# VectorE's modulation columns take their weight block one slab earlier

## The chip, the cores and the metric

The kernel runs on one core of one Trainium2 chip. The metric is the device time of one execution in microseconds (us). The time before is the median of three runs.

## The reference

Two blocks of a network, one after the other, each of two layers. Batch 1, 512 tokens of width 1024, and 256 context tokens beside them in the first block. All in float32.

The first block's layer `l`, cut to what matters here (the context goes the same way, with `c_ctx` in place of `c`; layer 1 leaves the context's output out):

```python
mx = jnp.split((jax.nn.silu(c) @ w_ada[l] + b_ada[l])[:, None, :], 6, axis=-1)
hx = modulate(rmsnorm(x, g_pre_mix[l]), mx[0], mx[1])          # h * (1 + scale) + shift
out_x, out_c = token_mixers(hx, hc, w_in[l], w_out[l], ...)
x = x + mx[2] * rmsnorm(out_x, g_post_mix[l])
hx = modulate(rmsnorm(x, g_pre_mlp[l]), mx[3], mx[4])
x = x + mx[5] * rmsnorm(jnp.square(jax.nn.relu(hx @ w_mlp1[l])) @ w_mlp2[l], g_post_mlp[l])
```

`w_ada[l]` is 1024 x 6144, `w_mlp1[l]` 1024 x 4096, `w_mlp2[l]` 4096 x 1024. The second block has the same kind of modulation, `mod = silu(c_2) @ ada_w_2[l] + ada_b_2[l]` with `ada_w_2[l]` 1024 x 3072, in front of three mixing branches, and no MLP.

## The kernel before

**Layout.** Activations lie transposed, features on the 128 partitions, tokens along the row. A matmul in full float32 is made of three faster ones: weights and activations are both split into a rounded part and the rest, and high x high, rest x high and high x rest are added in PSUM (L1104, L1105, L1106). A weight *slab* is up to 128 x 1024 numbers (512 KB). It comes from HBM into one of the six places of the ring `RG` (`RING = 6`; `RGR` is the same memory). ScalarE rounds it, half by half, into one of the two buffers `WHI` (L2321), GpSimd leaves the rest in place, in `RGR` (L2749).

**The transfer queue.** SyncE asks for all slabs in the order in which the schedule made them. For slab `i` it first waits until the last user of slab `i - 6` is done: a matmul (`matmuls`), or a column on VectorE (`columnsV`):

```python
if i >= RING:
    older = o.slabs[i - RING]["last"]
    e.wait_ge(*at("columnsV" if o.pieces[older]["kind"] == "column" else "matmuls", older))
e.dma_start(RG[:, i % RING, 0:n], dram["W"][i, :, 0:n])     # L1006
```

**The MLP.** Each layer of the first block does its MLP in four rounds of two stages: a `w_mlp1` stage (kind `relu2`, activations `HR`, 8 slabs) and a `w_mlp2` stage (kind `plus`, activations `HIDR`, 8 slabs). In layer 0 a slab is multiplied for 256 context tokens and then for 512 tokens (24 matmuls of each length, two pieces), in layer 1 for 512 tokens alone. After a `relu2` piece ScalarE empties the PSUM bank with a relu into `RLT` (L2483), VectorE squares it (L1861), ScalarE rounds the square into `HIDR` (L2485), VectorE makes the rest (L1863). After a `plus` piece VectorE adds the bank to `OUTF` (L1871 in the first round, L1874). Four PSUM banks serve in turn.

**The columns.** Part of the modulation is computed on VectorE during the MLPs. One column is 128 outputs of a modulation: the slab is a transposed block of `w_ada` or `ada_w_2`, 128 outputs by 1024 inputs, and VectorE multiplies it with the silu of `c`, spread over all partitions, and sums along the row. In layer 0 there are 48 columns with two products each, for `c` and for `c_ctx` (L1656, L1659); in layer 1 there are 36 with one (L1663). They are needed only after the MLP.

**What sets the order.** One list of steps is written by a schedule (`Order`), and each engine's program goes through it and takes the steps that concern it. After every piece `run` adds that piece's estimated time to `credit`; when `credit` reaches the period (8.0 in layer 0, 5.0 in layer 1), `filling` calls `next_column`. With estimates of 8.4 and 5.6 per slab this is once after each weight slab, behind its last evacuation. `next_column` puts a column's step into the list and makes the slab of a later one (`column`, which appends to `loaded`; `sums` holds those whose slab is not made yet). Slabs of weights and columns thus alternate in the ring. The weight slab after the one at work is made before the work on it begins. ScalarE's and GpSimd's rounding of a slab's halves (`split`) is put into the list by `place`, from estimates of when a buffer and a ring place are free. In layer 1 VectorE also makes tables of sine and cosine arguments between the pieces (`table`, L2050 to L2063).

Of the kernel before, what the change touches and what calls it, by code (L numbers as in the profile page):

```python
# [143 lines left out]
class Order:  # L144
# [88 lines left out]

    def next_column(self):

        if self.loaded and (len(self.loaded) > 1 or not self.sums):
            self.step("column", self.loaded.pop(0))
        if self.sums:
            self.column(*self.sums.pop(0))
# [2663 lines left out]
```

## Time and profile before

| | |
|---|---|
| runs | 3344.07, 3338.84, 3344.05 us; median 3344.05 |
| the profiled execution | 3338.16 us, its span 3336.40 us |
| mean granted TensorE clock | 0.945 |
| TensorE busy | 3000.8 us (90%) |
| VectorE busy | 1596.7 us (48%) |
| ScalarE busy | 1056.0 us (32%) |
| GpSimd busy | 1187.9 us (36%) |
| moved | 276.98 MB, mean 83 GB/s |

The profile is of one execution of the program. PE is TensorE's matmuls, PEld its weight loads, DVE VectorE, ACT ScalarE, POOL GpSimd, SP SyncE; SPq is SyncE's issuing of a transfer. Times count from the start of the span. L12 is line 12 of the kernel. A tile's buffer number is left out. The clock is the share of full speed that TensorE was granted. In layer 0 the MLP runs from 530 to 1153 us, in layer 1 from 1560 to 1994 us.

### The profile page before, as it was taken

The numbers are of one execution on the slowest core, as the hardware profiler recorded it, in microseconds if no ns is written. First come the engines' busy times: TensorE is split into PE (matmuls) and PEld (weight loads), VectorE is DVE, ScalarE is ACT, GpSimd is POOL, SyncE is SP. The second block draws the span as 40 slices with busy tenths as digits, with TensorE's granted clock in tenths as the row PEclk, the third lists the DMA queues.
The fourth block names the chain that finished last, engine by engine and source line by source line (L and its number), as shares of the span: only waits on it lengthen the run. The fifth ranks groups of instructions, "written<-read, shape, count | busy, mean of one in ns | idle before, by whom it ended". The sixth has DMA issues, their size and how long they took to land.

```text
span 3336.4 us, 41550 instructions
## 1 busy us (share of the span) xinstructions
PE 3000.8 (90%) x15908; PEld 2412.6 (72%) x15908; DVE 1596.7 (48%) x2851; ACT 1056.0 (32%) x1958; POOL 1187.9 (36%) x862
## 2 busy tenths in 40 slices
PE   7999788898899989968879899999989999999898
PEld 5788677777778867857657676777678767776786
DVE  4673535545555257344533214553482245544822
ACT  3224434121212231344222233233333322333332
POOL 1121142333333422214434452333255623332555
PEclk9999898999999989978989998999999989999999
DMA  5232011323233211103434321212112312221222
GB/s 202 90 138 76 13 55 53 102 101 109 94 114 107 66 57 63 58 23 101 145 106 154 119 89 67 74 64 64 61 60 73 93 64 70 64 70 57 62 75 67
DMA packets 78388, 276.98 MB, mean 83 GB/s; under 512 B 8544, under 2 KB 10848, under 8 KB 77936
## 3 DMA queue, kind: packets, MB, share of 16 engines
q1 hardware_dynamic: 75824, 268.91, 24.3%
q10 hardware_dynamic: 2368, 5.42, 0.4%
q8 instruction: 128, 2.10, 0.3%
q14 instruction: 68, 0.56, 0.1%
HBM read 272.19 MB, written 2.10 MB: 82 GB/s over the span
## 4 chain that ended last, share of the span: by engine, by line
PE 67%; DVE 15%; DMA 6%; ACT 5%; issue 4%; POOL 2%; SPq 0%; DVEq 0%; ACTq 0%; POOLq 0%
PE pb L1104 14%; PE pb L1105 14%; PE pb L1106 14%; DMA RG<-in_W_dram 6%; PE pb L1231 2%; DVE RLT L1861 2%; PE pb L1126 2%; PE pb L1128 2%; PE pb L1127 2%; PE pb L1143 1%; DVE AR L1822 1%; PE pb L1144 1%; PE pb L1145 1%; POOL RGR L2749 1%; PE pb L1189 1%
## 5 line engine op out<-in xcount | busy, mean ns | idle before, releaser
L2749 POOL TENSOR_TENSOR RGR<-RG,WHI 128x512 fp32r<-128x512 f32 x708 | 1002.5, 1426 | 1863.3 <-ACT WHI L2321 1862.3
L2321 ACT ACTIVATE WHI<-RG 128x512 fp32r<-128x512 f32 x708 | 432.5, 623 | 858.9 <-DMA RG<-in_W_dram 434.2
L1104 PE MATMUL pb<-HI,WHI 128*128 128x512 f32 (+1 forms) x880 | 374.8, 426 | 10.5 <-DVE LO L1750 4.9
L1106 PE MATMUL pb<-LO,WHI 128*128 128x512 f32 (+1 forms) x880 | 351.7, 400 | 0.0
L1105 PE MATMUL pb<-HI,RGR 128*128 128x512 f32 (+1 forms) x880 | 351.2, 399 | 0.0
L1104 PE MATMUL pb<-HR,WHI 128*128 128x512 f32 (+1 forms) x768 | 287.3, 374 | 68.0 <-POOL RGR L2749 61.6
L1104 PE MATMUL pb<-HIDR,WHI 128*128 128x512 f32 (+1 forms) x768 | 280.5, 365 | 42.4 <-POOL RGR L2749 17.1
L1106 PE MATMUL pb<-HR,WHI 128*128 128x512 f32 (+1 forms) x768 | 283.7, 369 | 0.0
L1105 PE MATMUL pb<-HR,RGR 128*128 128x512 f32 (+1 forms) x768 | 283.5, 369 | 0.0
L1105 PE MATMUL pb<-HIDR,RGR 128*128 128x512 f32 (+1 forms) x768 | 278.2, 362 | 0.0
L1106 PE MATMUL pb<-HIDR,WHI 128*128 128x512 f32 (+1 forms) x768 | 278.1, 362 | 0.0
L1861 DVE TENSOR_TENSOR RLT<-RLT 128x256 f32<-128x256 f32 (+1 forms) x96 | 98.2, 1023 | 270.0 <-ACT RLT L2483 269.4
L1104 PEld LDWEIGHTS pb<-HR,WHI 128*128 128x128 f32 x768 | 151.0, 197 | 105.7 <-issue 79.1
L1104 PEld LDWEIGHTS pb<-HI,WHI 128*128 128x128 f32 (+1 forms) x880 | 166.8, 190 | 77.9 <-issue 32.2
L1104 PEld LDWEIGHTS pb<-HIDR,WHI 128*128 128x128 f32 x768 | 147.0, 191 | 75.0 <-issue 28.4
L1106 PEld LDWEIGHTS pb<-LO,WHI 128*128 128x128 f32 (+1 forms) x880 | 166.5, 189 | 43.4
L1105 PEld LDWEIGHTS pb<-HI,RGR 128*128 128x128 f32 (+1 forms) x880 | 167.1, 190 | 38.4 <-issue 4.3
L1104 PE MATMUL pb<-HH,WHI 128*128 128x512 f32 (+1 forms) x464 | 170.8, 368 | 13.2 <-DVE HL L1750 12.1
L1106 PEld LDWEIGHTS pb<-HR,WHI 128*128 128x128 f32 x768 | 151.2, 197 | 24.0
L1105 PEld LDWEIGHTS pb<-HR,RGR 128*128 128x128 f32 x768 | 151.6, 197 | 22.7
L1105 PE MATMUL pb<-HH,RGR 128*128 128x512 f32 (+1 forms) x464 | 165.2, 356 | 0.0
L1106 PE MATMUL pb<-HL,WHI 128*128 128x512 f32 (+1 forms) x464 | 165.2, 356 | 0.0
(418 smaller groups left out, 5696.3 us busy)
## 6 DMA issues: line engine op xcount, KB each, us to landing
RG<-in_W_dram SPq DMA_DIRECT2D x504, 512.0 KB, 3.6
XCX<-in_xT_dram ACTq DMA_DIRECT2D x4, 512.0 KB, 11.8
out_dram<-XCX SPq DMA_DIRECT2D x8, 256.0 KB, 2.1
CS<-in_CST_dram ACTq DMA_DIRECT2D x1, 1027.0 KB, 4.8
XCC<-in_ctxT_dram SPq DMA_DIRECT2D x4, 256.0 KB, 13.7
AR<-in_VEC_dram ACTq DMA_DIRECT2D x1, 1024.0 KB, 6.3
CS<-in_CST_dram SPq DMA_DIRECT2D x1, 523.0 KB, 4.3
RG<-in_W_dram SPq DMA_DIRECT2D x2, 256.0 KB, 3.0
```

The costliest lines, as they stand in the source:

```text
L1104: e.matmul(out, hi[:, k, :], xh, start=k == order[0], stop=False)
L1105: e.matmul(out, lo[:, k, :], xh, start=False, stop=False)
L1106: i = e.matmul(out, hi[:, k, :], xl, start=False, stop=k == order[7])
L1126: e.matmul(out, xh[:, sl], hi[:, k, :], start=h == 0 and i0 % per == 0 and k == 0, stop=False)
L1127: e.matmul(out, xh[:, sl], lo[:, k, :], start=False, stop=False)
L1128: i = e.matmul(out, xl[:, sl], hi[:, k, :], start=False, stop=p["final"] and ends and k == nk - 1)
L1143: e.matmul(out, hi[:, k, :], xh, start=k == 0, stop=False)
L1144: e.matmul(out, lo[:, k, :], xh, start=False, stop=False)
L1231: m = e.matmul(sum_at(tag, c), squares_at(tag, i)[:, a:a + 128], ones[:, 0:1], start=k == 0 and c == first, stop=k == 7 and c == 5)
L1861: e.tensor_tensor(r, r, r, MUL).then_inc(*up("evacV", ("hidden", i)))
L2321: e.activation(WHI[:, u % 2, h * n:h * n + n], RG[:, s % RING, h * n:h * n + n], ACT.Copy).then_inc(*up("weightsA", (u, h)))
L2749: e.tensor_tensor(RGR[:, s % RING, sl], RG[:, s % RING, sl], WHI[:, u % 2, sl].bitcast(F32), SUB).then_inc(*up("weightsG", (u, h)))
```

## The change

`next_column` before put a column's step into the list only when a second slab was loaded behind it, or none was left to load. Now it takes the one that is loaded at every call, and then makes the next slab. The order in which slabs are made is the same.

```diff
     def next_column(self):
 
-        if self.loaded and (len(self.loaded) > 1 or not self.sums):
+        if self.loaded:
             self.step("column", self.loaded.pop(0))
         if self.sums:
             self.column(*self.sums.pop(0))
```

## Rows read from the trace of the kernel before

**Rows 1.** The page, part 4: the chain, share of the span by engine, by line

```profile
PE 67%; DVE 15%; DMA 6%; ACT 5%; issue 4%; POOL 2%; SPq 0%; DVEq 0%; ACTq 0%; POOLq 0%
...
```

**Rows 2.** Waits of SyncE's queue, 600 to 1060 us (layer 0's columns)

```profile
engine line waited for: us in total, times, longest us
SPq L1006 <- DVE RG L1659: 424.1, 46, 12.6
SPq L1006 <- PE pb L1106: 4.5, 12, 0.4
```

**Rows 3.** Waits of SyncE's queue, 1590 to 1865 us (layer 1's columns)

```profile
SPq L1006 <- DVE RG L1663: 245.3, 35, 9.3
SPq L1006 <- PE pb L1106: 0.4, 2, 0.2
```

**Rows 4.** Waits of all engines, 600 to 1060 us

```profile
ACT WHI L2321 <- DMA RG<-in_W_dram: 242.9, 43, 10.0
```

**Rows 5.** Windows of the MLPs' stages

```profile
core 0: us, PE busy (x) PEld busy (x) DVE busy (x) ACT busy (x) POOL busy (x), PEclk, DMA share, GB/s
558.64:608.37 49.73, 47.99 (x266) 41.21 (x266) 19.73 (x28) 14.05 (x27) 14.32 (x10) 1.00 0.20 64
608.37:1085.47 477.10, 427.79 (x2305) 366.27 (x2305) 251.06 (x332) 101.59 (x197) 172.97 (x98) 0.96 0.31 105
1085.47:1152.80 67.33, 67.33 (x385) 58.73 (x384) 9.58 (x17) 18.22 (x33) 32.28 (x28) 1.00 0.21 63
...
1580.96:1613.51 32.55, 28.48 (x121) 22.35 (x121) 16.98 (x20) 9.35 (x17) 13.29 (x9) 1.00 0.30 97
1613.51:1904.18 290.67, 243.51 (x961) 188.30 (x961) 106.48 (x142) 69.63 (x121) 125.80 (x82) 0.94 0.40 136
...
1904.18:1993.50 89.32, 89.32 (x385) 72.14 (x384) 16.59 (x24) 32.84 (x55) 48.27 (x38) 1.00 0.31 95
```

**Rows 6.** Windows inside two `w_mlp2` stages with columns, layer 0 and layer 1

```profile
645.32:687.19 41.87, 41.87 (x241) 36.50 (x239) 20.86 (x30) 5.46 (x10) 17.07 (x9) 1.00 0.37 126
1762.62:1789.82 27.20, 27.20 (x118) 21.91 (x117) 8.56 (x15) 5.77 (x10) 12.68 (x10) 1.00 0.53 186
```

**Rows 7.** The chain in order of time, layer 1: start us, us, what

```profile
1697.76 1.24 DVE RG L1663 x2
...
1699.38 4.42 DMA RG<-in_W_dram
...
1704.97 1.44 DVE RLT L1861
...
1706.44 0.64 ACT HIDR L2485
...
1707.71 1.22 DVE RG L1663
```

**Rows 8.** ScalarE in order of time, layer 0

```profile
start us, us, engine line op out<-in xcount [idle before <-releaser]
581.35 0.60 ACT L2483 ACTIVATE RLT<-pb 128x512 f32<-128x512 f32 x1 [2.10 <-PE pb L1106]
...
587.81 0.42 ACT L2485 ACTIVATE HIDR<-RLT 128x256 fp32r<-128x256 f32 x1 [3.25 <-DVE RLT L1861]
592.94 0.63 ACT L2321 ACTIVATE WHI<-RG 128x512 fp32r<-128x512 f32 x1 [4.72 <-DMA RG<-in_W_dram]
593.48 0.58 ACT L2483 ACTIVATE RLT<-pb 128x512 f32<-128x512 f32 x1
```

**Rows 9.** VectorE in order of time, layer 0

```profile
583.98 1.22 DVE L1656 SCALAR_TENSOR_TENSOR CS<-RG,AR 128x1024 f32<-128x1024 f32 x1
...
587.36 0.41 DVE L1861 TENSOR_TENSOR RLT<-RLT 128x256 f32<-128x256 f32 x1
...
594.10 1.47 DVE L1861 TENSOR_TENSOR RLT<-RLT 128x512 f32<-128x512 f32 x1 [5.41 <-ACT RLT L2483]
```

**Rows 10.** VectorE in order of time, layer 1: one call of `table`

```profile
1606.24 3.20 DVE L2058 SCALAR_TENSOR_TENSOR TAB<-TMP,TAB 128x512 f32<-128x512 f32 x3
1609.47 0.43 DVE L2060 TENSOR_SCALAR TAB<-TAB 128x512 f32<-128x512 f32 x1
```

**Rows 11.** The line L1656: duration ns min/median/max, first and last start us

```profile
L1656 DVE SCALAR_TENSOR_TENSOR CS<-RG,AR x48: 1210/1218/2290, 584.0 to 1058.7; 128x1024 f32<-128x1024 f32 x48
```

**Rows 12.** The chain in order of time, layer 0, 620 to 634 us

```profile
626.00 5.98 DMA RG<-in_W_dram
```

## The prediction, made before the change was run

> **What bounds the kernel now.** I read the page's chain first, then what the transfer queue waits for, then the stretches of the two MLPs, then one turn of the loop inside them.
>
> The chain lies on TensorE for 67% of the span, but 6% of the span is weight blocks in flight and 15% VectorE [rows 1]. In a kernel that mostly multiplies neither should be there. The queue's own waits say why. In layer 0's columns SyncE stood 424.1 us over 46 requests waiting for the second product of a column (L1659), and 4.5 us for TensorE [rows 2]; in layer 1's, 245.3 us over 35 for L1663 and 0.4 us for TensorE [rows 3]. So VectorE's columns time the requests for weights. ScalarE, which has to round each weight block before anything later in its program, stood 242.9 us over 43 waits for a transfer in the first of these stretches [rows 4].
>
> What it costs TensorE. A stage is 8 weight slabs, with 48 matmuls each in layer 0 and 24 in layer 1 (the windows count one more at an edge). Without columns 8 slabs took 67.33 us in layer 0, 8.416 each, and 16 took 89.32 us in layer 1, 5.583 each, at a granted clock of 1.00. With columns six stages of layer 0 (48 slabs) took 477.10 us at 0.96, and five of layer 1 (40 slabs) 290.67 us at 0.94 [rows 5]. The columns themselves do not slow TensorE: in two stretches of w_mlp2 with a column per slab it was busy all the time, beside transfers of 126 and 186 GB/s [rows 6]. The loop is in w_mlp1.
>
> One turn of it in layer 1 [rows 7]: the column at 1697.76 ends 1.24 later; the weight block asked for then is in flight for 4.42 us from 1699.38; ScalarE rounds its first half and only then empties the PSUM bank; VectorE squares at 1704.97, ScalarE rounds the hidden value at 1706.44, the next column begins at 1707.71. The turn is 9.95 us, against 5.58 for the slab's matmuls. It closes because SyncE asks in slab order: in front of each weight block stands a column block, and that one's place in the ring is the one whose column has just been done. In layer 0 the first stall is the same: ScalarE began its short copy at 587.81 (0.42 us) and then waited 4.72 us for the transfer [rows 8].
>
> **The change, part by part.** No instruction and no transfer is added, removed or reordered in its own kind; only the column steps move among the steps.
>
> (a) All 84 columns come one slab earlier, each behind the same kind of evacuation; the last slab of each run of columns has none now. VectorE does the same work per slab, so by itself this is 0.
>
> (b) The place of a column block comes free one slab earlier. SyncE's wait for it is then over long before the wait of the weight block behind it, which is for the matmuls of three weight slabs back. The request therefore goes out at the end of those matmuls, not after the square, the split and the products that follow them: in layer 0 at about 581.4, where ScalarE's evacuation starts, and not at 587.4 [rows 8, 9], so 6 us earlier. Behind this new last wait stand all later requests, columns' blocks too; they have slabs of time. What was 4.8 us of every turn (0.4 to issue, 4.42 in flight) lies beside matmuls.
>
> (c) A column's block is still asked for three slabs before its column; VectorE waits for none.
>
> (d) The splits of a few weight slabs behind the last columns, whose places held column blocks, may be put a step or two earlier: 0.
>
> What is late next? Layer 1: without the flight the turn is 1704.97 to 1707.71 and 1.24 for the column, 3.98 us [rows 7], under 5.58. Asked for at the end of a slab's matmuls the block lands 4.8 us later and is wanted before the next slab's evacuation, 5.58 later: 0.8 to spare. Layer 0: from the column to the short square 3.38, to ScalarE's copy 0.45, that copy 0.42, rounding of the half to the evacuation 0.54, to the square 0.62 [rows 8, 9], square to rounding 1.47 and on to the column 1.27 as in layer 1 [rows 7]. Sum 8.15, under 8.42 though only by 0.3. TensorE is next in both.
>
> **The sum**, from the windows [rows 5]:
> layer 0, six stages: 477.10 - 48 x 8.416 = 73.1;
> layer 0, from 558.64: one long piece (5.6) and 5 slabs want 47.7, took 49.73: 2.0;
> layer 1, five stages: 290.67 - 40 x 5.583 = 67.4;
> layer 1, from 1580.96: 5 slabs want 27.9, took 32.55: 4.6.
> Together 147.1. TensorE's idle time in it is 1.7 + 49.3 + 4.1 + 47.2 = 102.3; the other 45 are matmuls that ran slower, at a mean clock of 0.94 to 0.96 after the stops, between the levels of 1.2 and 2.4 GHz. Both should come back, since every window without stops has 1.00 [rows 5, 6].
>
> The Trainium skill (TensorE: Matmul & The Clock Gate, "HAM oscillation — how this bites in real kernels") says the same of waits for transfers between groups of matmuls, that each can put the clock to its lower level. By it the gain is near 147, by idle time alone near 102; the trace's clock columns agree with it.
>
> Taken off: layer 1 makes its position tables on VectorE between these columns. One call costs 3.20 + 0.43 us [rows 10], the loop can catch up 1.6 us a slab (5.58 - 3.98), and four PSUM banks stand between. Bounds 0 and 3.6 for each of two calls in w_mlp1; I take 3 us. Another 2 us for the turns from stage to stage. Gain 142.
>
> The profiled execution took 3338.16 us, its span 3336.40: 3338.16 - 142 = 3196. The median shown, 3344.05, lies 5.9 above that execution and two of the three runs lie at it, so I put the result at 3344 - 142 = **3202 us**.
>
> **Rivals.** *VectorE becomes the bound in layer 0.* The first product of a column takes 1.218 us in the median and 2.290 at most [rows 11]. If every one meets GpSimd's subtraction in the new order, the turn is 8.15 + 1.07 = 9.22, 0.8 over TensorE, in the 24 slabs of w_mlp1 with a column: 19 us, so 3221. Against it: the phase of rounding, subtraction and column follows from the same two ScalarE steps as before, and with an unhurried square (no stall) there is more room.
>
> The Trainium skill (SBUF — State Buffer, "SBUF: two separate sides") has VectorE operations with two inputs from SBUF and GpSimd's reads take turns at one pair of ports, each for a whole instruction. By it the long value is the rule wherever the two meet, and the sum is 19 us less; the median shows that this product rarely meets one today.
>
> *The block lands late in layer 1.* The spare is 0.8 us; one flight in the chain took 5.98 [rows 12], and 0.4 + 5.98 is 0.8 more than 5.58. If all 36 slabs are like it, 29 us stay, with the clock's share (147 to 102) 42: 3244. Against it: that flight was one of four blocks asked for close together, and 186 GB/s was held without a stop [rows 6].
>
> *The clock stays where it is*: 102 - 5, so 3247. Against it: 1.00 wherever there was no stop.
>
> *The change does not do what it says.* The weight block has its own wait for matmuls; if that ends when the column did, the time is 3344. Against it: 6 us lie between the two in layer 0, and TensorE is named for 4.5 us of 429 [rows 2].
>
> *Slower*: the column reaches VectorE before its block has landed, and squares and evacuations queue behind it. It is asked for three slabs ahead, 16.7 us in layer 1, and needs 4.8. This decides from a flight of 16 us on; with a slab then 2 us longer at 84 columns it is 168 us, so 3512. Nothing in these stretches is near it.
>
> **How the numbers follow.** Forecast 0.66 (own range 3189, all 147 back from the fastest runs, to 3212), VectorE 0.12, late block 0.09, clock 0.05, no effect 0.05, slower 0.03. The range, 3189 to 3245, takes in the first three, 0.87. What a measurement of this kernel can tell from no change is about 0.2%, 6.7 us. Faster 0.92, same 0.05, slower 0.03.
>
> **What would show it.** Right: SyncE's waits name TensorE and hardly L1659 or L1663; ScalarE's 242.9 us for transfers fall below 30; columns of w_mlp1 in layer 1 stand 5.6 us apart, not 10, and in layer 0 8.4; stages of 67 to 69 and 45 to 47 us at clock 1.00; nothing differs after the MLPs. Wrong: columns 9 us apart in layer 0 (VectorE); ScalarE waiting 1 us a slab in layer 1 (flight); SyncE still released by VectorE (no effect); VectorE idle before L1656 or L1663 for a transfer (slower).

## The result, and the profile after

The changed kernel takes 3200.68 us in the median (3192.79 to 3203.02, four runs) against 3341.45 (3334.02 to 3344.07, four runs: the three listed above and one more): a ratio of 0.9578, 95% interval 0.9554 to 0.9602. The forecast was 3202. The profiled execution took 3198.54 us, its span 3196.7, where the one before had 3336.4. A second measurement, with the last three experiments, gave 3200.18 (ratio 0.9573, 0.9558 to 0.9588).

The page of the kernel after, its chain by engine:

```profile
PE 79%; DVE 12%; ACT 4%; issue 3%; POOL 1%; DMA 0%; SPq 0%; DVEq 0%; ACTq 0%; POOLq 0%
```

Transfers had 6% of the chain [rows 1] and now have none that shows; TensorE went from 67% to 79%. The number of instructions and the bytes moved are the same.

The windows of the same stages after (us, busy time by engine, clock, share of the transfer engines, GB/s):

```profile
561.64:610.92 49.28, 49.28 (x267) 42.43 (x267) 25.89 (x39) 16.55 (x32) 18.44 (x12) 0.97 0.28 90
610.92:1014.91 403.99, 403.99 (x2305) 352.34 (x2304) 225.60 (x320) 105.06 (x192) 165.60 (x97) 1.00 0.39 121
1014.91:1082.25 67.34, 67.34 (x385) 58.73 (x384) 9.57 (x17) 18.23 (x33) 32.31 (x28) 1.00 0.21 63
1511.11:1539.12 28.01, 28.01 (x120) 22.65 (x121) 18.86 (x23) 10.69 (x20) 14.67 (x9) 1.00 0.45 150
1539.12:1763.17 224.05, 224.05 (x962) 180.53 (x960) 97.87 (x139) 71.71 (x120) 135.55 (x82) 1.00 0.54 172
1763.17:1852.76 89.59, 89.59 (x385) 72.25 (x384) 16.61 (x24) 32.84 (x55) 48.26 (x38) 1.00 0.31 94
```

Against the windows before [rows 5]: the six stages of layer 0 went from 477.10 to 403.99 us, that is 48 slabs at 8.416, the rate without columns to the last digit; the five of layer 1 from 290.67 to 224.05, 40 slabs at 5.60. TensorE is busy in the whole of each window, and in these two its clock is 1.00 where it was 0.96 and 0.94; only the first window, in front of them, has 0.97. Line by line the MLPs became 0.45 + 73.11 - 0.01 + 4.54 + 66.62 - 0.27 = 144.4 us shorter. The spans differ by 139.7; the other 4.7 lie outside the windows, which this one execution went through more slowly: 3.0 before the first, 0.7 between the layers and 1.0 after the last. The parts between the two MLPs vary from 407 to 415 us in the executions profiled here, whichever rule the columns follow.

Who makes SyncE's queue wait, after, 575 to 1035 us and then 1515 to 1790 us:

```profile
SPq L1006 <- DVE RG L1659: 228.7, 48, 5.8
SPq L1006 <- PE pb L1106: 198.7, 55, 8.1
...
SPq L1006 <- PE pb L1106: 136.2, 46, 6.1
SPq L1006 <- DVE RG L1663: 109.3, 36, 6.5
```

Before, VectorE had nearly all of it [rows 2, 3]. Now the queue waits twice per slab: the column block's request waits for a column, and the weight block's behind it for TensorE's matmuls. It is the second that ends last before a weight block, as VectorE and ScalarE show for the slabs printed here. VectorE in order of time, the end of a column in layer 0 and of one in layer 1:

```profile
701.29 0.08 DVE L1659 DVE_READ_ACCUMULATOR RG<-RG,AR 128x1 f32 x1
...
1604.81 0.08 DVE L1663 DVE_READ_ACCUMULATOR RG<-RG,OUTF 128x1 f32 x1
```

The columns end at 701.37 and 1604.89. TensorE is done with its slab where ScalarE's evacuation starts, at 703.70 and 1606.57 in the rows below, so the column's place is free 2.3 and 1.7 us ahead of the other wait. VectorE's share is no sign of harm any more, since it only times the blocks of columns as long as it ends first.

ScalarE in order of time, after, one slab of `w_mlp1` in layer 0 and then one in layer 1:

```profile
701.74 0.42 ACT L2485 ACTIVATE HIDR<-RLT 128x256 fp32r<-128x256 f32 x1 [3.25 <-DVE RLT L1861]
702.07 0.62 ACT L2321 ACTIVATE WHI<-RG 128x512 fp32r<-128x512 f32 x1
703.70 0.60 ACT L2483 ACTIVATE RLT<-pb 128x512 f32<-128x512 f32 x1 [1.02 <-PE pb L1106]
...
1605.72 0.63 ACT L2321 ACTIVATE WHI<-RG 128x512 fp32r<-128x512 f32 x1 [2.17 <-DMA RG<-in_W_dram]
1606.57 0.60 ACT L2483 ACTIVATE RLT<-pb 128x512 f32<-128x512 f32 x1 [0.22 <-PE pb L1106]
```

In layer 0 the rounding follows the short copy at once, where it had waited 4.72 us for the transfer [rows 8], and ScalarE is the one that waits for TensorE, 1.02 us a slab. In layer 1 it still waits for the block, here 2.17 us, but the block comes before TensorE is done with the slab, and the last thing waited for is TensorE again, by 0.22 us. ScalarE's waits for transfers in layer 1 thus still come to 75.0 us over 32 (1511 to 1790 us), where they were 177.9 over 36 (1590 to 1865 us), and they cost TensorE nothing.

### The profile page after: what moved, and what is told of

The parts are those of the page before. It is cut to its first block, busy times and chain, and to the rows that moved or that the text cites. A ratio compares the mean times of both kernels' runs of the same rounds, so it can differ in the third digit from the quotient of the medians.

```text
span 3196.7 us, 41550 instructions
## 1 busy us (share of the span) xinstructions
PE 2962.0 (93%) x15908; PEld 2395.7 (75%) x15908; DVE 1571.0 (49%) x2851; ACT 1065.7 (33%) x1958; POOL 1196.3 (37%) x862
## 4 chain that ended last, share of the span: by engine, by line
PE 79%; DVE 12%; ACT 4%; issue 3%; POOL 1%; DMA 0%; SPq 0%; DVEq 0%; ACTq 0%; POOLq 0%
PE pb L1104 18%; PE pb L1106 17%; PE pb L1105 17%; PE pb L1231 2%; PE pb L1126 2%; PE pb L1127 2%; PE pb L1128 2%; PE pb L1143 1%; DVE AR L1822 1%; PE pb L1144 1%; PE pb L1145 1%; PE pb L1189 1%; PE pb L1239 1%; PE pb L1159 1%; PE pb L1047 1%
## 5 line engine op out<-in xcount | busy, mean ns | idle before, releaser
L1104 PE MATMUL pb<-HR,WHI 128*128 128x512 f32 (+1 forms) x768 | 277.0, 361 | 8.1 <-DVE HR L1750 5.6
L1106 PE MATMUL pb<-HR,WHI 128*128 128x512 f32 (+1 forms) x768 | 277.3, 361 | 0.0
L1105 PE MATMUL pb<-HR,RGR 128*128 128x512 f32 (+1 forms) x768 | 276.5, 360 | 0.0
L1106 PE MATMUL pb<-HIDR,WHI 128*128 128x512 f32 (+1 forms) x768 | 275.0, 358 | 0.0
L1104 PE MATMUL pb<-HIDR,WHI 128*128 128x512 f32 (+1 forms) x768 | 273.9, 357 | 0.0
L1104 PEld LDWEIGHTS pb<-HR,WHI 128*128 128x128 f32 x768 | 145.9, 190 | 32.8 <-issue 6.1
L1106 PEld LDWEIGHTS pb<-HR,WHI 128*128 128x128 f32 x768 | 146.2, 190 | 23.1
L1105 PEld LDWEIGHTS pb<-HIDR,RGR 128*128 128x128 f32 x768 | 144.3, 188 | 23.4
```

What stands on the lines that cost most here:

```text
L1104: e.matmul(out, hi[:, k, :], xh, start=k == order[0], stop=False)
L1105: e.matmul(out, lo[:, k, :], xh, start=False, stop=False)
L1106: i = e.matmul(out, hi[:, k, :], xl, start=False, stop=k == order[7])
```

## The experiments

Each number "before" below is the median of the runs of the kernel before on the same chip: 3342.23 us for the first four experiments, 3340.62 for the last three and the repeat.

**1. The new rule in layer 0 alone, and 2. in layer 1 alone.**

```diff
-        if self.loaded and (len(self.loaded) > 1 or not self.sums):
+        if self.loaded and (self.period == 8.0 or len(self.loaded) > 1 or not self.sums):   # 2: period == 5.0
```

The lines are set against the kernel before; the comment is not in the code.

> The new rule in layer 0 alone (48 columns), the old one in layer 1. Theory (the weights' requests are held by the ring place of a late column, in both layers for the same reason): the gain splits by the stages' excess, 73 to 75 of some 145 us here, so about 3268 against 3341; layer 0's stages 67.3 us, layer 1's 69 and 54 as before. Rival (one shared cause outside these stages, such as the clock being raised by the whole run being denser, or the few moved splits behind the last columns): the parts would not add up; one layer alone would bring nearly all or nearly nothing.

> The new rule in layer 1 alone (36 columns). Theory: 71 us of the gain, about 3270; layer 1's stages 44.8 us, layer 0's as before. The two parts add up to the whole within some 5 us. Rival: as in the run of layer 0 alone, they do not add up.

Measured: 3265.58 us (ratio 0.9771, 0.9755 to 0.9787) and 3271.45 us (0.9787, 0.9768 to 0.9806). The gains are 76.7 and 70.8, together 147.4, beside 141 for both at once (experiment 3, on the same chip as the two, has both and 143.9); the prediction's windows had 75.1 and 72.0. They add up to the 141 within 6.6 us, a little more than the 5 expected. Neither half brings nearly all or nearly nothing, so nothing that the two layers share is behind the gain. With the rule in layer 0 alone that layer's six stages read, in the windows,

```profile
611.85:1015.85 404.00, 404.00 (x2305) 352.67 (x2304) 225.59 (x320) 105.03 (x192) 165.45 (x97) 1.00 0.39 121
```

and SyncE's queue in layer 1, 1520 to 1800 us,

```profile
SPq L1006 <- DVE RG L1663: 249.5, 36, 9.5
SPq L1006 <- PE pb L1106: 0.4, 2, 0.2
```

so the one layer stands as in the kernel after and the other as in the kernel before [rows 3]. With the rule in layer 1 alone it is the other way round: that layer's five stages took 223.38 us at a clock of 1.00, and layer 0's six 474.78 at 0.96.

**3. The column of the block that the same call makes.** The lines are set against the changed kernel.

```diff
     def next_column(self):
-        if self.loaded:
-            self.step("column", self.loaded.pop(0))
         if self.sums:
             self.column(*self.sums.pop(0))
+        if self.loaded:
+            self.step("column", self.loaded.pop(0))
```

> Goes one slab further: the block that a call has just made is also the one whose column is put into the list, so a place is held one slab less again. Theory: the weights' requests are released by TensorE already and land in time, so nothing more is gained: within 5 us of the changed kernel, about 3200. A column's block is then asked for some two slabs ahead of its column, 11 us in layer 1 against 4 to 5 of flight, so VectorE still waits for none. Rival (the gain goes on with each slab that a column comes earlier, because it is the moment of the column on VectorE that counts): some tens of us faster than 3200. Second rival (VectorE reaches the column before its block): slower than 3200, VectorE idle before L1656 and L1663 for a transfer.

Measured: 3198.30 us (0.9574, 0.9555 to 0.9593), against 0.9573 to 0.9578 for the change itself. No more is gained. SyncE's queue, 575 to 1035 us:

```profile
SPq L1006 <- PE pb L1106: 417.9, 55, 8.1
SPq L1006 <- DVE CS L1656: 1.5, 1, 1.5
```

VectorE times hardly anything any more, and it makes no difference: what counts is whether the place is free when the weight block behind it could go. The step from two slabs held to one was worth 141 us, the next nothing. VectorE never waited for a block in that stretch (its waits name TensorE and ScalarE only), nor in layer 1, 1500 to 1800 us, where the one transfer it waited for, 1.1 us, is that of the positions; so the rival in which the column comes too early is refuted even one slab further on.

**4. The kernel before, with layer 0's second product cut short.** It multiplies 64 of the 1024 inputs, so the context's modulation is not computed.

```diff
-                e.scalar_tensor_tensor(out=w, in0=w, scalar=1.0, in1=SPREAD[0][:, 1, :], op0=MUL, op1=MUL,
+                e.scalar_tensor_tensor(out=w[:, 0:64], in0=w[:, 0:64], scalar=1.0, in1=SPREAD[0][:, 1, 0:64], op0=MUL, op1=MUL,
```

> The kernel before, with the second product of layer 0's columns cut to 64 of 1024 inputs; so the modulation for the context is wrong, and VectorE has 2.1 us less per column. Theory: in the old order the column's time on VectorE is part of the turn, so w_mlp1's slabs come 2.1 us closer (12.2 to about 10.1, TensorE's own is 8.4); 55% of layer 0's excess of 73 us goes, 40 us, so about 3300. Rival (VectorE's work is beside the path and only the number of bytes or the moment of the request against the matmuls counts): no change, 3341.

Measured: 3317.02 us (0.9926, 0.9910 to 0.9943), 25 us less, not 40. The direction supports the theory, VectorE's time is part of the old turn; the size was wrong, and its trace says why. VectorE in order of time:

```profile
708.96 1.22 DVE L1656 SCALAR_TENSOR_TENSOR CS<-RG,AR 128x1024 f32<-128x1024 f32 x1
...
710.22 1.19 DVE L1659 SCALAR_TENSOR_TENSOR RG<-RG,AR 128x64 f32<-128x64 f32 x1
```

GpSimd in order of time:

```profile
705.82 1.29 POOL L2749 TENSOR_TENSOR RGR<-RG,WHI 128x512 fp32r<-128x512 f32 x1 [5.80 <-ACT WHI L2321]
708.98 2.35 POOL L2749 TENSOR_TENSOR RGR<-RG,WHI 128x512 fp32r<-128x512 f32 x1 [1.88 <-ACT WHI L2321]
```

The line L1659 (duration in ns, min/median/max):

```profile
L1659 DVE SCALAR_TENSOR_TENSOR RG<-RG,AR x48: 224/1186/1199, 588.7 to 1035.2; 128x64 f32<-128x64 f32 x48
```

The product over 64 numbers takes 1.19 us, though the shortest of the 48 took 0.224, at 627.50 us, when GpSimd had nothing to do from 625.30 to 632.41. It ends at 711.41, just after GpSimd's subtraction at 711.33. The subtraction in turn began with the first product and took 2.35 us instead of the 1.29 that it takes alone in this trace: it got going when the first product ended. So the product cut to a sixteenth gave back 1.0 us, not 2.1: the next column, at 720.18, comes 11.22 us after this one, where the kernel before has some 12.2. One of 3.8 us of excess per turn is 26% of layer 0's 73, some 20, and 25 were measured. The windows have them: the six stages took 451.60 us against 477.10 [rows 5], 25.5 less. Of these, 8.0 came out of the first `w_mlp1` stage alone, 79.47 us against 87.44, which is 1.0 us for each of its 8 slabs.

**5 and 6. The changed kernel, with the first product made twice, and three times.** The same sum is written again.

```diff
                 e.scalar_tensor_tensor(out=PRODUCT, in0=w, ..., accum_out=MODS[i][:, p["j"], 0:1]).then_inc(*up("columnsV"))
                 e.wait_ge(*now("columnsV"))
+                e.scalar_tensor_tensor(out=PRODUCT, in0=w, ..., accum_out=MODS[i][:, p["j"], 0:1]).then_inc(*up("columnsV"))
+                e.wait_ge(*now("columnsV"))
```

> The changed kernel with each column's first product in layer 0 made twice (the same sum, written again): 1.22 + 0.08 us more of VectorE per column. It asks how far VectorE's loop is from being the bound. The prediction's sum for the turn (8.15 us against 8.42) leaves 0.3 us, so 1.0 us too much in the 24 slabs of w_mlp1: 25 us, about 3225. What the changed kernel's trace shows instead (ScalarE waits 1.02 us for TensorE in each such slab, the squares take 0.69, not 1.47) leaves 1.0 us, so 0.3 us too much in 24 slabs: 7 us, about 3208, unless the slower turn brings back the slow squares. Rival (VectorE was the bound's cause all along): much more, 1.3 us in all 48 columns, 62 us.

> The same with the first product made three times: 2.6 us more per column. By the trace's slack of 1.0 us: 1.6 us too much in 24 slabs, 38 us, and a few more for the clock: about 3240 to 3255. By the prediction's sum (0.3 us): 2.3 us in 24 slabs, 55 us, and the clock: about 3260 to 3275. In w_mlp2's stages nothing in either case, since ScalarE has nothing there that waits for VectorE.

Measured: 3208.83 us (0.9602, 0.9589 to 0.9615) and 3240.86 (0.9699, 0.9686 to 0.9712), so 8.7 and 40.7 us over the changed kernel on that chip. Both lie near what the trace's slack of 1.0 us gave: 7 us were expected for one more product, and 38 and a few more for two; the prediction's own slack of 0.3 us gave 25 and 55 and more. The way there was not the one that this sum took, so that the numbers came out so close is partly luck. ScalarE in order of time, with one product more:

```profile
703.50 0.42 ACT L2488 ACTIVATE HIDR<-RLT 128x256 fp32r<-128x256 f32 x1 [4.95 <-DVE RLT L1864]
703.82 0.62 ACT L2324 ACTIVATE WHI<-RG 128x512 fp32r<-128x512 f32 x1
704.34 0.58 ACT L2486 ACTIVATE RLT<-pb 128x512 f32<-128x512 f32 x1
...
712.82 0.42 ACT L2488 ACTIVATE HIDR<-RLT 128x256 fp32r<-128x256 f32 x1 [4.95 <-DVE RLT L1864]
```

VectorE in order of time, the square between them:

```profile
704.95 1.46 DVE L1864 TENSOR_TENSOR RLT<-RLT 128x512 f32<-128x512 f32 x1 [0.58 <-ACT RLT L2486]
```

Its windows of two stages of `w_mlp2` with one of `w_mlp1` between them:

```profile
745.29:817.55 72.26, 69.41 (x386) 59.99 (x384) 51.45 (x73) 12.06 (x20) 31.12 (x18) 0.98 0.38 123
817.55:885.05 67.50, 67.50 (x386) 58.81 (x384) 52.60 (x72) 21.17 (x44) 25.50 (x15) 1.00 0.34 118
885.05:957.29 72.24, 69.39 (x386) 60.00 (x384) 51.44 (x73) 12.07 (x20) 30.82 (x18) 0.98 0.40 124
```

The turn is 712.82 - 703.50 = 9.32 us, 0.9 over TensorE's 8.42, ScalarE no longer waits for TensorE, and the long square takes 1.46 us again: the slow squares, which the expectation had named as the one thing that could upset its sum, came back. Yet the `w_mlp1` stage has 67.50 us: TensorE ran ahead of the others, and four banks and two buffers are what could let it; no run varied them. The debt, 8 turns of 0.9 or 7.2 us, is collected at the next stage, whose first matmuls need the last hidden values: 72.2 instead of 67.3, 4.9 us. Two stages paid so, 9.8 us of the 10.9 by which the six (414.92 us) are over 404.0. With two more products the turn is 10.6 us, with the slow square too, and both kinds of stage are late:

```profile
684.42:759.88 75.46, 71.25 (x386) 61.65 (x384) 61.59 (x86) 21.17 (x44) 25.74 (x15) 0.95 0.33 111
759.88:834.02 74.14, 70.28 (x386) 60.76 (x384) 62.42 (x91) 12.06 (x20) 30.83 (x18) 0.95 0.36 115
```

That `w_mlp2`'s stages would lose nothing in either run, as experiment 6's expectation has it, was wrong: in both runs it is where a `w_mlp1` stage's lag is paid.

**7. The kernel before, with half of each column block of layer 0.** The transfer brings 512 of 1024 inputs, and both products run over them twice, so that VectorE has the same work; layer 0's columns are not computed rightly.

```diff
-            n = slab["item"][3] * (slab["item"][5])
+            n = slab["item"][3] * (slab["item"][5]) // (2 if slab["item"][0] == "w_ada:T" else 1)
...
+                half = w[:, 0:512].unsqueeze(1).to_broadcast([128, 2, 512])
+                (both products read half and write PRODUCT, as [128, 2, 512])
```

> The kernel before, with half of each column block of layer 0 transferred (512 of 1024 inputs, and both products run over this half twice, so VectorE has the same work and layer 0's columns are wrong). It takes bytes out of the flight alone. Theory (the flight of column block and weight block together is part of the turn in the old order): a pair took 4.42 us where a single block lands in 3.2 to 3.5, so half a block less is some 0.5 us per turn, of an excess of 3.8: 10 us, about 3332, and the flight after a column 3.9 instead of 4.4. Rival (VectorE's part alone sets the turn): no change.

Measured: 3328.91 us (0.9962, 0.9949 to 0.9974), 11.7 less. Two flights after a column in its chain, in order of time:

```profile
702.68 4.46 DMA RG<-in_W_dram
...
714.91 3.74 DMA RG<-in_W_dram
```

These two differ, but over the six stages the weight blocks landed 3.8 us after their request in the median, where the kernel before has 4.5. The six stages took 462.56 us against 477.10 [rows 5], 14.5 less, so the gain lies where the blocks were halved. The theory asked for some 10 us and the rival for none: the flight is in the old turn as well.

**The repeat.** 

> The changed kernel on the same chip as the three others, to compare them with. Every theory: about 3201.

3200.18 us (0.9573, 0.9558 to 0.9588).

## Why the prediction was right, point by point

*The cause.* That late columns held ring places in front of weight blocks, and that the 4.8 us from request to landing was thereby inside the turn, held. The windows show the stops gone; the two halves add up; VectorE's time (experiment 4) and the flight (7), each changed by itself, move the old kernel in the direction and, with the contention counted, by about the size; one slab further (3) nothing is left to gain. What no run did is to free the place earlier and leave the columns where they were, by a longer ring for instance.

*The sum.* 147.1 by windows, 144.4 in the trace. Layer 0's six stages: 73.1 forecast, 73.11 measured. Layer 1's five: 67.4 and 66.6. Layer 1's first: 4.6 and 4.5. Layer 0's first window: 2.0 and 0.45. There the sum set "one long piece and 5 slabs" equal to 47.7 us, but the window takes 49.28 with TensorE busy throughout, at a clock of 0.97: it begins behind a stop of TensorE, 2.03 us, that lies before the first column. The 1.7 us of stops inside it went as forecast, and 1.6 us of slower matmuls came in their place, which the window before, behind a stop of 1.99 us, did not have. The 5 us taken off for tables and turns between stages were not there: layer 1's first stretch, with table calls in it, was at 28.0 us. So the windows promised 2.7 us too much, the 5 us taken off were 5 too many, the other parts took 4.7 more in the profiled execution, and the fourth run before put its median 2.6 us under the 3344 that the sum started from. That all this left the forecast 1.3 us off is luck; that the gain was 141 where 142 was forecast rests on the windows, which were right to 3 us.

*The clock.* All of it came back, as the forecast took it: 102 of the 147 were idle time, and the gain was 141. The rival with 102 alone is refuted. That the other 45 were all slow clock is not shown: 0.04 of 477 us and 0.06 of 291 us [rows 5] make some 36, an estimate, and what the other 9 of TensorE's busy time were stays open. They came back too. And "every window without stops has 1.00" has one exception after, the first, with 0.97.

*What is next.* The prediction gave VectorE's and ScalarE's turn in layer 0 8.15 us with 0.3 to spare. The trace has 1.02, ScalarE's wait for TensorE. The step that was off is the square to rounding, 1.47: it came from turns in which ScalarE's rounding, held by the transfer, set GpSimd off just ahead of the square (subtraction from 710.17 to 711.47, square from 710.54, in the kernel before). Without the stop the subtraction is over before the square (702.82 to 704.11, square from 704.33), which takes 0.69. The slow value is still there to fall back into: experiment 5 has 8.15 + 1.3 = 9.45 by the prediction's terms and 9.32 by its trace. The rival "VectorE becomes the bound" was therefore rightly unlikely, and its price of 19 us for 0.8 us a turn was too high: at 0.9 us a turn experiment 5 paid 8.7, since some 2.3 us of a stage's lag of 7.2 did not reach TensorE, and the last `w_mlp1` stage with columns had no debt to pay on. Its condition, a first product at 2.29 us, did not occur: all 48 lie between 1.215 and 1.221.

*The flight in layer 1.* Forecast spare 0.8 us; the trace's smallest is 0.22. The term left out is the rounding of the block's first half, which stands between its landing and the evacuation: 0.54 us in layer 0's rows [rows 8], and 0.8 less 0.54 is 0.26. The block landed as forecast, 4.8 us after the slab's matmuls (1600.97 to 1605.72). It was the nearest of the rivals.

*The signs.* Four held: ScalarE's waits for transfers in layer 0 went from 242.9 us to none; the columns of `w_mlp1` stand 8.4 us apart in layer 0 and 5.6 in the mean in layer 1; the stages take 67.3 and 44.8 us at clock 1.00 (45 to 47 were named for layer 1); behind the MLPs 1.0 us differs. Nor does VectorE wait for a block. Two signs misled. "SyncE's waits name TensorE and hardly L1659 or L1663" was false, with 228.7 and 109.3 us, and by the text's own words that would have meant no effect. And ScalarE still waits for the block by more than 1 us a slab in layer 1, which was to mean a late flight: it is only early there. The step that failed is in (b): the queue's wait for the place is not "over long before", but 2.3 and 1.7 us before. The queue reaches it while the column is still to come and waits there, then waits again for the matmuls. What decides is which of the two ends last, and that was forecast rightly.

## What to carry to other kernels

In a ring that is filled in order, a place held one step too long is paid for by whatever stands behind it in the queue, not by its own user; look at which wait of the queue ends last before the late transfer, not at the longest total. Count how many steps a block lies finished before it is used: taking it a step earlier cost nothing here and moved a whole flight out of the loop. A neighbouring stage with nothing but matmuls gives the rate at which the loop should run, and the difference of the two, with the clock in it, was a forecast good to 3 us in 147.

## What the runs showed of the hardware

GpSimd's subtraction and VectorE's product, both with two inputs from SBUF, took turns as whole instructions: a product of 64 numbers lasted 1.19 us because a subtraction of 128x512 was in front of it, and 0.22 us when none was; the subtraction lasted 2.35 instead of 1.29 us behind a product of 1.22. The Trainium skill (SBUF — State Buffer, "SBUF: two separate sides") states such a lock on one pair of ports; the traces agree, and they show that an order can repeat exactly: in all 48 columns of the changed kernel the second product pays (2.18 to 2.20 us), never the first (1.22), while in the kernel before the first paid at times (2.29 at most [rows 11]). So a VectorE product cut to a sixteenth gave back less than half its time.

TensorE's clock: layer 0's six stages before, with 49.3 us of stops, the longest of them 3.1 us, had a mean of 0.96, and layer 1's five, with 47.2 us of stops, 0.94. The windows without stops had 1.00, under 186 GB/s of transfers as well, but for one with 0.97 right behind a stop of 2.03 us. TensorE's busy time in the windows with stops was 45 us over the rate without them, beside 102 us of the stops themselves; some 36 of the 45 are what the granted clock accounts for, an estimate from its means.
